# Neighbourhood values with high and low parts side by side as weights, two query tiles at a time, and the fillers' second units in other steps

## The chip, the cores and the metric

One NeuronCore of a Trainium2 chip runs the whole program: TensorE (matmuls, writing to PSUM), VectorE, ScalarE and GpSimd work beside each other, and SyncE issues the DMAs in one in-order queue. Engines meet by semaphores. The metric is the device time of one execution in microseconds (us), the median of several runs; lower is better.

## The reference

Two layers of a mixer with three branches run over 128 context and 1024 latent tokens (1152 in all), width 1024. The branch that matters here is neighbourhood attention with 8 heads of 64:

```python
s_loc = einsum('bhrqd,bhriwd->bhrqiw', qg, kg) * scale + bias   # 8 x 16 window, clamped at the borders
s_loc = where(col_ok, s_loc, NEG_INF)
s_ctx = einsum('bhrqd,bhnd->bhrqn', qg, k_ctx) * scale
p = softmax(concatenate([s_loc, s_ctx], -1))
o = einsum('bhrqiw,bhriwd->bhrqd', p_loc, vg) + einsum('bhrqn,bhnd->bhrqd', p_ctx, v_ctx)
```

Each layer starts with `mod = silu(c) @ w_mod + b_mod`, which scales, shifts and gates the normalised input, and one projection `h @ w_in` feeds queries, keys, values and gates of all branches. All is float32.

## The kernel before

**Exactness.** Every product of two float32 operands is made of three matmuls in the faster f32r form: each operand is split into a high part (a copy rounded to f32r, by ScalarE) and a low part (the rest, by VectorE or GpSimd), and high x high, high x low and low x high are summed in PSUM.

**The neighbourhood phase.** A layer handles its 8 heads as 4 pairs `p`; `u` numbers the pairs of both layers, 0 to 7. A pair has 9 query tiles of 128 tokens, steps `t` = 0 to 8 (8 is the context tile, `LT`). A query tile attends to its own key tile, the two beside it and the cached context tile `TILES`: 3 key tiles for t = 0 and 7, 4 for 1 to 6, 1 for 8. In a step, TensorE turns the probabilities of tile t (`probs_t`, L896 to L902, banks 6 and 7 of PSUM), computes the scores of tile t+1 (L770, L779), runs a unit, multiplies values by probabilities (`values`, L905 to L914, bank 4), and may run a second unit. ScalarE copies the turned probabilities to `pth` (`highs`) and takes exponentials of tile t+1 (`exps`); VectorE makes `ptl` (`lows`), adds the bias, normalises (`biased`, `normed`) and multiplies the output by the gate (`gated`, L1722).

The values of both heads of a pair stand side by side as weights, 128 keys x (64 + 64) channels, `vhi` and `vlo`; the moving operand is the probabilities of both heads, 256 columns. The result is 128 x 256, of which `gated` reads the two 64 x 128 blocks that belong together.

**Units and fillers.** A unit is 24 matmuls of 384 columns (L731), a third of one 128-channel chunk of the big projection. Each head pair carries 5 filler chunks, 15 units numbered 0 to 14 here: q, k, a gate, v and a gate (`qkgvg`) for the next pair, five gates for the last pair. `na_steps` (L109) deals them out: two units in each of steps 0 to 5, one in steps 6 to 8. ScalarE evacuates a unit (`evacuate`), and after a chunk's third unit copies the high part of a later weight chunk (L1143); GpSimd makes the low part (L1999).

**Modulations.** In layer 0, each of steps 0 to 7 of each pair also runs one of the next 32 modulation products: `modulation` (L790) on the buffer `mraw` before the unit, ScalarE copies the row, `modulation_sums` folds it (L796) after the unit. `mraw` is one buffer of 512 KB.

**SyncE's queue.** SyncE walks over the pair's five fillers. For filler j it first issues a weight load (L495), then modulation loads up to a fixed number, each behind the use of the load before, and then what the chunk's result needs:

```python
for j, c in enumerate(fillers(l, "na", p)):
    weights_to(CHUNK[c] + 3)
    if l + 1 < DEPTH:
        mod_to(MOD_STEPS * p + (3, 4, 6, 7, 8)[j])
    keep_streaming(c)
```

`keep_streaming` (L511) waits for the evacuation of the chunk's third unit, `unit_evac(c, NC - 1)`, if the chunk is k, v or a gate, and issues its store (L518, L523). `MOD_STEPS` is 8, so the load for step 7 is issued at j = 4, behind the store of the fourth filler, whose third unit is unit 11.

Of the kernel before, what the change touches and what calls it, by code (L numbers as in the profile page):

```python
# [8 lines left out]
F32 = mybir.dt.float32  # L9
# [202 lines left out]
def build(nc, x_in, cache_na_k, cache_na_v, cache_diff_k, cache_diff_v, cvec, norm_g, w_mod,  # L212
# [66 lines left out]
    kh = pl("kh", [P, TK], F32R)  # L279
    kl = pl("kl", [P, TK], F32R)  # L280
    vhi = pl("vhi", [P, TILES + 1, P], F32R)
    vlo = pl("vlo", [P, TILES + 1, P], F32R)
    vraw = pl("vraw", [P, P])
    gst_at = pl.at
# [113 lines left out]
    def group(g):  # L398

        return ps[:, 3 * g:3 * g + NC, 0:CH]  # L400

    def by_chunk(ap):
        return ap.rearrange("p (c n) -> p c n", n=CH)
# [4 lines left out]
        un_done u_evac z_tanh z_evac  # L408
        na_s na_b na_e na_p na_pt na_pth na_ptc na_pv na_o df_s df_m df_e df_p df_pt df_pth df_ptc df_pv df_o
        f_store0 f_store1 u_pair pair_copied folded x_done q_done q_copied f_hi f_lo f_ctx  # L410
# [69 lines left out]
    with nc.Block() as block:  # L480
# [3 lines left out]
        def _(sp):  # L484
# [70 lines left out]
            for l in range(DEPTH):  # L555
# [9 lines left out]
                for p in range(HEADS):  # L565
# [23 lines left out]

                    sp.wait_ge(S.na_o, TILES * (u + 1))  # L590
                    sp.dma_start(outs_dram[0, p], obuf[:]).then_inc(S.o_store, 16)
# [106 lines left out]
        def _(pe):  # L698
# [157 lines left out]
            for l in range(DEPTH):  # L856
# [17 lines left out]
                for p in range(HEADS):  # L874
# [46 lines left out]
                    unit(z, 0)  # L921
                    pe.wait_ge(S.na_o, TILES * u)
                    values_to_rows(n, v, 1, 4)
# [8 lines left out]
                    for t, units in enumerate(na_steps(l, p)):  # L932
                        probs_t(t, 0)
                        probs_t(t, 1)
                        if t + 1 < TILES:
                            scores(t + 1)
                        mod = l + 1 < DEPTH and t < MOD_STEPS
                        if mod:
                            modulation(MOD_STEPS * p + t)
                        unit(*units[0])  # L940
                        if mod:
                            modulation_sums(MOD_STEPS * p + t)
                        values(t)
                        if len(units) > 1:
                            unit(*units[1])
# [39 lines left out]
                job(("u", l, "fn", 0), hhi, hlo)  # L985
                pe.wait_ge(S.na_o, TILES * HEADS * (l + 1))
                if l + 1 < DEPTH:
# [141 lines left out]
        def _(act):  # L1129
# [69 lines left out]

            def cached_high(n):  # L1200
                act.wait_ge(S.vc_load, 16 * (n + 1))
                fn(vhi[:, TILES, :], vraw[:], ACT.Copy).then_inc(S.vc_hi, 1)

            def value_high(n, i, bank):

                a, b = 4 * i, min(4 * i + 4, TILES)
                act.wait_ge(S.v_done, 3 * n + i + 1)
                fn(vhi[:, a:b, :], ps[:, bank, 0:(b - a) * P].rearrange("p (t n) -> p t n", n=P), ACT.Copy
                   ).then_inc(S.v_hi, 1)
# [62 lines left out]
            for l in range(DEPTH):  # L1272
# [26 lines left out]
                for p in range(HEADS):  # L1299
# [10 lines left out]
                    def highs(t, e):  # L1310

                        n = len(na_tiles(t))
                        act.wait_ge(S.na_pt, u0 + 2 * t + e + 1)
                        if e == 0 and t >= 2:

                            act.wait_ge(S.na_pv, TILES * u + t - 1)
                        fn(pth[:, t % 2, 0:n, e, :], ps[:, 6 + e, 0:n * P].rearrange("p (t n) -> p t n", n=P), ACT.Copy  # L1317
                           ).then_inc(S.na_pth, 1)

                    if p:  # L1320
                        act.wait_ge(S.na_pv, TILES * u)
                    cached_high(n)
                    value_high(n, 0, 5)
                    if p:
                        act.wait_ge(S.na_o, TILES * u)
                    evacuate(z, 0)
                    value_high(n, 1, 4)
                    evacuate(z, 1)
                    value_high(n, 2, 5)
# [214 lines left out]
        def _(dve):  # L1544
# [84 lines left out]
            for l in range(DEPTH):  # L1629
# [45 lines left out]

                def value_low(n, i, bank):

                    a, b = 4 * i, min(4 * i + 4, TILES)
                    dve.wait_ge(S.v_hi, 3 * n + i + 1)
                    v.tensor_tensor(vlo[:, a:b, :], ps[:, bank, 0:(b - a) * P].rearrange("p (t n) -> p t n", n=P),  # L1680
                                    vhi[:, a:b, :].bitcast(F32), ALU.subtract).then_inc(S.v_lo, 1)

                for p in range(HEADS):
# [24 lines left out]
                    def lows(t, e):  # L1708

                        n = len(na_tiles(t))  # L1710
                        dve.wait_ge(S.na_pth, u0 + 2 * t + e + 1)
                        v.tensor_tensor(ptl[:, t % 2, 0:n, e, :], ps[:, 6 + e, 0:n * P].rearrange("p (t n) -> p t n", n=P),  # L1712
                                        pth[:, t % 2, 0:n, e, :].bitcast(F32), ALU.subtract).then_inc(S.na_ptc, 1)
# [12 lines left out]
                    value_low(n, 0, 5)  # L1726
                    silu_unit(z, 0)
                    value_low(n, 1, 4)
# [4 lines left out]
                    value_low(n, 2, 5)  # L1733
                    normed(0, 0)
                    normed(0, 1)
                    silu_unit(z, 2)
                    for t in range(TILES):
# [7 lines left out]
                        if l + 1 < DEPTH and t < MOD_STEPS:  # L1745
# [242 lines left out]
        def _(pool):  # L1988
# [26 lines left out]
            for l in range(DEPTH):  # L2015
# [8 lines left out]

                def cached_low(n):
                    pool.wait_ge(S.vc_hi, n + 1)
                    g_.tensor_tensor(vlo[:, TILES, :], vraw[:], vhi[:, TILES, :].bitcast(F32), ALU.subtract
                                     ).then_inc(S.vc_lo, 1)
# [5 lines left out]
                for p in range(HEADS):  # L2034
                    n, cs = n0 + p, fillers(l, "na", p)
                    split_to(SPLIT_NO[cs[0]] + 1)
                    cached_low(n)
                    split_to(SPLIT_NO[cs[-1]] + 2)
# [152 lines left out]
```

## Time and profile before

| | us |
|---|---|
| median of 3 runs | 2887.7 |
| lowest, highest | 2886.08, 2890.15 |
| the profiled execution | 2886.48 |
| its span in the trace | 2884.7 |

The neighbourhood phases lie at about 100 to 522 us (layer 0) and 1514 to 1930 us (layer 1). In the rows below a line names the start and duration in us, the engine, the source line, the operation and its tiles (out<-in), and shapes. Matmuls are pipelined: the recorded duration of one is longer than the distance between two starts, and the distance is what one costs when they follow each other.

### The profile page before, as it was taken

The page shows a single profiled execution, that of the slowest core. Times are in us where ns is not written, and L with a number is a line of the kernel's source. Part 1 is how long each engine was busy: PE and PEld are TensorE (multiplying, and loading weights), DVE is VectorE, ACT ScalarE, POOL GpSimd, SP SyncE. Part 2 cuts the span into 40 slices and gives each one's busy share as a digit, 9 for nine tenths or more (in the row PEclk, how much of TensorE's full clock was granted, in tenths as well). Part 3 has the DMA queues.
Part 4 walks back from the last instruction along what each step waited for, and adds up shares of the span by engine and source line. Part 5 has one row for each costly group of instructions (what it writes and reads, how often), then busy time and mean ns, then how long its engine had stood idle before and what let it go on. Part 6 is the DMA issues. An engine that isn't in the chain of part 4 may idle for free.

```text
span 2884.7 us, 43952 instructions
## 1 busy us (share of the span) xinstructions
PE 2824.3 (98%) x18284; PEld 2712.9 (94%) x18284; DVE 1341.0 (46%) x2349; ACT 1070.2 (37%) x1963; POOL 614.3 (21%) x312
## 2 busy tenths in 40 slices
PE   6999999999999999999999999999999999999998
PEld 4999999999999989999999999999999989999997
DVE  4343444233657575446344434423156567554643
ACT  4333333322444444422343433423234444533132
POOL 0221221133121212122431221213222221211141
PEclk9999999999999999999999999999999999999999
DMA  5332233202111112254422120221211111215532
GB/s 213 113 113 74 105 100 111 84 26 84 41 42 47 49 33 96 88 205 139 127 88 67 67 84 32 84 83 35 75 34 48 49 42 47 88 48 188 167 108 94
DMA packets 83702, 246.57 MB, mean 85 GB/s; under 512 B 9136, under 2 KB 30128, under 8 KB 82480
## 3 DMA queue, kind: packets, MB, share of 16 engines
q1 hardware_dynamic: 83504, 243.76, 24.9%
q8 instruction: 145, 2.38, 0.3%
q14 instruction: 53, 0.43, 0.0%
HBM read 189.72 MB, written 54.00 MB: 84 GB/s over the span
## 4 chain that ended last, share of the span: by engine, by line
PE 90%; DVE 5%; ACT 2%; DMA 1%; issue 1%; SPq 0%; DVEq 0%; POOL 0%; POOLq 0%; ACTq 0%
PE ps L731 45%; PE ps L714 19%; PE ps L834 6%; PE ps L770 5%; PE ps L914 3%; PE ps L1057 3%; PE ps L1048 2%; PE ps L902 2%; PE ps L977 1%; DVE e L1882 1%; DVE stat L1865 1%; ACT e L1456 1%; DMA wmod<-w_mod 1%; DVE aTl L1889 1%; PE ps L790 1%
## 5 line engine op out<-in xcount | busy, mean ns | idle before, releaser
L731 PE MATMUL ps<-hhi,whi 128*128 128x384 f32 x2640 | 915.7, 347 | 5.7 <-DVE obuf L1897 3.3
L731 PE MATMUL ps<-hhi,wlo 128*128 128x384 f32 x2640 | 885.6, 335 | 0.0
L731 PE MATMUL ps<-hlo,whi 128*128 128x384 f32 x2640 | 883.1, 335 | 0.0
L1999 POOL TENSOR_TENSOR wlo<-wraw,whi 128x1024 fp32r<-128x1024 f32 (+1 forms) x188 | 415.9, 2213 | 2010.3 <-ACT whi L1143 2010.3
L731 PEld LDWEIGHTS ps<-hhi,whi 128*128 128x128 f32 x2640 | 499.5, 189 | 37.2 <-issue 23.4
L731 PEld LDWEIGHTS ps<-hlo,whi 128*128 128x128 f32 x2640 | 496.4, 188 | 0.9
L731 PEld LDWEIGHTS ps<-hhi,wlo 128*128 128x128 f32 x2640 | 495.4, 188 | 0.0
L1143 ACT ACTIVATE whi<-wraw 128x1024 fp32r<-128x1024 f32 (+1 forms) x188 | 174.5, 928 | 224.4 <-PE ps L714 206.5
L1465 ACT ACTIVATE aTh<-ps 128x512 fp32r<-128x512 f32 (+1 forms) x200 | 96.5, 482 | 273.3 <-PE ps L1048 273.3
L1712 DVE TENSOR_TENSOR ptl<-ps,pth 128x512 fp32r<-128x512 f32 (+1 forms) x144 | 82.1, 612 | 246.8 <-ACT pth L1317 246.6
L1865 DVE TENSOR_REDUCE stat<-ps 128x1 f32<-128x1152 f32 x144 | 176.6, 1231 | 13.8 <-PE ps L770 13.4
L1456 ACT ACTIVATE e<-ps,stat 128x1152 f32<-128x1152 f32 x144 | 162.4, 1128 | 55.0 <-DVE stat L1865 55.0
L1168 ACT ACTIVATE gst<-ps 128x384 f32<-128x384 f32 x144 | 70.5, 490 | 262.9 <-PE ps L731 262.9
L1889 DVE TENSOR_TENSOR aTl<-ps,aTh 128x512 fp32r<-128x512 f32 (+1 forms) x200 | 108.4, 542 | 103.6 <-ACT aTh L1465 102.8
L1307 ACT ACTIVATE sn<-sn,stat 128x512 f32<-128x512 f32 (+1 forms) x144 | 95.8, 665 | 112.5 <-DVE stat L1697 106.5
L714 PE MATMUL ps<-omh,whi 128*128 128x384 f32 x576 | 132.4, 337 | 0.0
L714 PE MATMUL ps<-omh,wlo 128*128 128x384 f32 x576 | 131.6, 336 | 0.0
L714 PE MATMUL ps<-oml,whi 128*128 128x384 f32 x576 | 131.5, 336 | 0.0
L1048 PE MATMUL ps<-ident,e 128*128 128x128 f32 x584 | 100.5, 279 | 12.2 <-DVE aTl L1889 9.7
L770 PE MATMUL ps<-kh,qh 64*128 64x384 f32 (+2 forms) x560 | 103.8, 366 | 0.0
L714 PEld LDWEIGHTS ps<-omh,whi 128*128 128x128 f32 x576 | 103.1, 188 | 0.5
L714 PEld LDWEIGHTS ps<-omh,wlo 128*128 128x128 f32 x576 | 103.3, 188 | 0.0
(217 smaller groups left out, 4788.5 us busy)
## 6 DMA issues: line engine op xcount, KB each, us to landing
wraw<-w_in SPq DMA_DIRECT2D x128, 512.0 KB, 4.3
gates_dram<-gst SPq DMA_DIRECT2D x48, 576.0 KB, 3.0
gth<-gates_dram SPq DMA_DIRECT2D x48, 576.0 KB, 4.7
mraw<-w_mod SPq DMA_DIRECT2D x32, 512.0 KB, 3.9
wraw<-w_branch SPq DMA_DIRECT2D x48, 256.0 KB, 2.8
bias<-rpb SPq DMA_DIRECT2D x8, 1280.0 KB, 6.0
outs_dram<-obuf SPq DMA_DIRECT2D x16, 576.0 KB, 4.0
oraw<-outs_dram SPq DMA_DIRECT2D x16, 576.0 KB, 3.8
```

Source lines behind the costliest of these rows:

```text
L714: x = mm(ps[:, at + n, 0:CH], a[:, s % 2, k, :], b[k][:, n * CH:(n + 1) * CH], start=(k == 0 and a is whi and b is mhi), stop=(k == kt - 1 ...
L731: x = mm(ps[:, bank, 0:CH], a[:, s % 2, k, :], b[:, k, n * CH:(n + 1) * CH], start=(k == 0 and a is whi and b is hhi), stop=(k == KT - 1 a ...
L770: x = mm(out, a[r, t * P:(t + 1) * P], b[r, k0:k1], start=(i == 0), stop=(i == 2))
L834: x = mm(ps[:, bank, 0:CH], a[:, k, :], b[:, k, n * CH:(n + 1) * CH], start=(k == 0 and a is hi and b is hhi), stop=(k == KT - 1 and a is lo))
L1048: x = nc.tensor.transpose(ps[:, DF_TURN_BANK[h][t], j * P:(j + 1) * P], e1[:, t % 2, kt * P:(kt + 1) * P], ident[:])
L1143: fn(halves(s)[0][:, 0:kt, :], wraw[:, n % 2, 0:kt, :], ACT.Copy).then_inc(S.w_hi, 1)
L1307: fn(sn[:, e, 0:nk], sn[:, e, 0:nk], ACT.Exp, bias=stat[:, e, 1:2], accum_out=stat[:, e, 3:4]).then_inc(S.na_e, 1)
L1456: fn(out if t == LT else by_chunk(out), group(m) if t < LT else ps[:, 3 * m, 0:nk], ACT.Exp, bias=stat[:, t % 2, m:m + 1], accum_out=stat[ ...
L1465: fn(aTh[:, 4 * g:4 * g + w, (t % 2) * P:(t % 2 + 1) * P], ps[:, DF_TURN_BANK[h][t], 0:w * P].rearrange("p (t n) -> p t n", n=P), ACT.Copy ...
L1865: v.tensor_reduce(stat[:, t % 2, m:m + 1], group(m) if t < LT else ps[:, 3 * m, 0:TC], AX.XY if t < LT else AX.X, ALU.max, negate=True).th ...
L1889: v.tensor_tensor(aTl[at], ps[:, DF_TURN_BANK[h][t], 0:w * P].rearrange("p (t n) -> p t n", n=P), aTh[at].bitcast(F32), ALU.subtract).then ...
L1999: g_.tensor_tensor(lo[:, 0:kt, :], wraw[:, n % 2, 0:kt, :], hi[:, 0:kt, :].bitcast(F32), ALU.subtract).then_inc(S.w_lo, 1)
```

## The change

**Weights and matmuls.** `vhi` and `vlo` become one tensor for this phase, `vparts`: for each key tile 256 columns in four quarters, head 0 high, head 0 low, head 1 low, head 1 high. A matmul now takes the 128 columns of one head (its high and low part) as weights and one part of that head's probabilities, of two query tiles together, as the moving operand. `values(pair)` therefore runs once for steps 0 and 1, 2 and 3, 4 and 5, 6 and 7, at the odd step, and once for step 8. Key tiles that only one of the two query tiles sees are multiplied with 128 columns, the others with 256. The product low x low, which was left out, is now summed too. `pth` and `ptl` hold 9 slots of two query tiles, instead of two buffers.

**Outputs.** High and low sums of a head stand in different halves of the partitions. ScalarE copies one half to the new `vsum` (`spilled`), VectorE adds the other half and multiplies by the gate (`gated`), for two tiles at once, at the even step after. `na_o` and `na_pv` count 5 per head pair (`NA_OUTS`) instead of 9.

**Units.** `NA_TWO` places the second units in steps 0, 2, 3, 4, 6 and 8: the steps hold 2,1,2,2,2,1,2,1,2 units instead of 2,2,2,2,2,2,1,1,1. SyncE's loop is unchanged.

```diff
+NA_TWO = (0, 2, 3, 4, 6, 8)
+NA_OUTS = LT // 2 + 1
+
+
 def na_steps(l, p):
 
     units = [(c, n) for c in fillers(l, "na", p) for n in range(NC)]
-    more, steps = len(units) - TILES, []
+    steps = []
     for t in range(TILES):
-        steps.append([units.pop(0) for _ in range(2 if t < more else 1)])
+        steps.append([units.pop(0) for _ in range(2 if t in NA_TWO else 1)])
...
+def turned_order(t):
+
+    tiles = na_tiles(t)
+    return [0, 1, 3, 2] if t % 2 and len(tiles) == 4 else [*range(len(tiles))]
+
+
+def first_slot(t):
+
+    return 1 if t % 2 or t == 0 else 0
...
+    vparts = nc.alloc_sbuf_tensor_at("vparts", [P, TILES + 1, 2 * P], F32R, offset=v_at)
...
-    pth = pl("pth", [P, 2, 4, 2, P], F32R)
-    ptl = pl("ptl", [P, 2, 4, 2, P], F32R)
+    pth_at = pl.at
+    pth = pl("pth", [P, 9, 2, P], F32R)
+    ptl = pl("ptl", [P, 9, 2, P], F32R)
     csilp = pl("csilp", [P, KT, 32])
-    mrow4 = pl("mrow4", [P, P])
+    mrow4 = nc.alloc_sbuf_tensor_at("mrow4", [P, P], F32, offset=pth_at + TILE_B)
+    vsum = pl("vsum", [P, 2 * P])
...
+        return vparts[:, a:b].rearrange("p t (q n) -> p t q n", n=P // 2)[:, :, 0:4:3, :]
...
+        return vparts[:, a:b].rearrange("p t (q n) -> p t q n", n=P // 2)[:, :, 1:3, :]
...
-                        for j in range(len(na_tiles(t))):
-                            x = nc.tensor.transpose(ps[:, 6 + e, j * P:(j + 1) * P], sn[:, e, j * P:(j + 1) * P], ident[:])
+                        for i, j in enumerate(turned_order(t)):
+                            x = nc.tensor.transpose(ps[:, 6 + e, i * P:(i + 1) * P], sn[:, e, j * P:(j + 1) * P], ident[:])
...
-                    def values(t):
-
-                        pe.wait_ge(S.na_ptc, u0 + 2 * t + 2)
-
-                        if t:
-                            pe.wait_ge(S.na_o, TILES * u + t)
-                        tiles = na_tiles(t)
-                        for j, vtile in enumerate(tiles):
-                            for a, b in ((vhi, pth), (vlo, pth), (vhi, ptl)):
-                                x = mm(ps[:, 4, 0:2 * P], a[:, vtile, :], b[:, t % 2, j], start=(j == 0 and a is vhi and b is pth),
-                                       stop=(j == len(tiles) - 1 and b is ptl))
+                    def values(pair):
+
+                        t = 2 * pair
+                        pe.wait_ge(S.na_ptc, u0 + 2 * min(t + 1, LT) + 2)
+
+                        if pair:
+                            pe.wait_ge(S.na_o, NA_OUTS * u + pair)
+                        if t == LT:
+                            tiles = [(0, LT, 0, P)]
+                        else:
+                            tiles = [(1, t, 0, 2 * P), (2, t + 1, 0, 2 * P), (3, TILES, 0, 2 * P)]
+                            tiles += [(0, t - 1, 0, P)] if t else []
+                            tiles += [(4, t + 2, P, 2 * P)] if t + 2 < LT else []
+                        for e in range(2):
+                            for slot, vtile, a, b in tiles:
+                                for part in (pth, ptl):
+                                    x = mm(ps[:, 4, 2 * P * e + a:2 * P * e + b], vparts[:, vtile, e * P:(e + 1) * P],
+                                           part[:, 4 * e + slot].rearrange("p q n -> p (q n)")[:, a:b],
+                                           start=(slot == tiles[0][0] and part is pth), stop=(slot == tiles[-1][0] and part is ptl))
                         x.then_inc(S.na_pv, 1)
...
-                        values(t)
+                        if t % 2 or t == LT:
+                            values(t // 2)
...
+                    def spilled(pair):
+
+                        w = 2 * P if pair < LT // 2 else P
+                        act.wait_ge(S.na_pv, NA_OUTS * u + pair + 1)
+                        if pair:
+                            act.wait_ge(S.na_o, NA_OUTS * u + pair)
+                        for e in range(2):
+                            own, other = slice(64 * e, 64 * e + 64), slice(64 - 64 * e, 128 - 64 * e)
+                            x = fn(vsum[own, 0:w], ps[other, 4, 2 * P * e:2 * P * e + w], ACT.Copy)
+                        x.then_inc(S.na_spilled, 1)
...
                         highs(t, 0)
                         highs(t, 1)
+                        if t and t % 2 == 0:
+                            spilled(t // 2 - 1)
...
-                        for c, i in units:
+                        for of, (c, i) in enumerate(units):
                             raw_free(c, i)
                             evacuate(c, i)
+                            if t == LT and of == 0:
+                                spilled(LT // 2)
...
-                    def gated(t):
-
-                        dve.wait_ge(S.na_pv, TILES * u + t + 1)
-                        if t == 0 and n:
+                        at = (slice(None), slice(4 * e + first_slot(t), 4 * e + first_slot(t) + n), t % 2 if t < LT else 0)
+                        v.tensor_tensor(ptl[at], ps[:, 6 + e, 0:n * P].rearrange("p (t n) -> p t n", n=P),
+                                        pth[at].bitcast(F32), ALU.subtract).then_inc(S.na_ptc, 1)
+
+                    def gated(pair):
+
+                        w = 2 * P if pair < LT // 2 else P
+                        dve.wait_ge(S.na_spilled, NA_OUTS * u + pair + 1)
+                        if pair == 0 and n:
                             dve.wait_ge(S.o_store, 16 * n)
                         for e in range(2):
-                            r = slice(64 * e, 64 * e + 64)
-                            x = v.tensor_tensor(obuf[r, P * t:P * t + P], ps[r, 4, P * e:P * e + P],
-                                                zs[r, P * t:P * t + P], ALU.mult)
-                        x.then_inc(S.na_o, 1)
-
-                    value_low(n, 0, 5)
+                            own = slice(64 * e, 64 * e + 64)
+                            v.tensor_tensor(vsum[own, 0:w], ps[own, 4, 2 * P * e:2 * P * e + w], vsum[own, 0:w], ALU.add)
+                        dve.drain()
+                        at = slice(2 * P * pair, 2 * P * pair + w)
+                        v.tensor_tensor(obuf[:, at], vsum[:, 0:w], zs[:, at], ALU.mult).then_inc(S.na_o, 1)
...
-                        gated(t)
+                        if t and t % 2 == 0:
+                            gated(t // 2 - 1)
+                    gated(LT // 2)
```

ScalarE, layer 0, second head pair, before: from the evacuation of unit 9 (`vT`) at the end of step 4 to `exps` in step 7. `pth` is `highs`, `sn` is `exps`, `mrow` the modulation's row, `vT`, `qraw`, `gst` the results of v, q and gate units, `whi` a weight chunk's high part.

```order
L1172 ACTIVATE vT<-ps 128x384
L1317 ACTIVATE pth<-ps 128x4x128 x2
L1307 ACTIVATE sn,stat<-sn,stat 128x512 x2
L1341 ACTIVATE mrow_100<-ps 128x128
L1172 ACTIVATE vT<-ps 128x384 x2
L1143 ACTIVATE whi<-wraw 128x1024
L1317 ACTIVATE pth<-ps 128x4x128 x2
L1307 ACTIVATE sn,stat<-sn,stat 128x384 x2
L1341 ACTIVATE mrow_100<-ps 128x128
L1168 ACTIVATE gst_93<-ps 128x384
L1317 ACTIVATE pth<-ps 128x3x128 x2
L1307 ACTIVATE sn,stat<-sn,stat 128x128 x2
```

And after: steps 6 and 7 of the same pair.

```order
L1365 ACTIVATE pth<-ps 128x4x128 x2
L1378 ACTIVATE vsum<-ps 64x256 x2
L1354 ACTIVATE sn,stat<-sn,stat 128x384 x2
L1402 ACTIVATE mrow_101<-ps 128x128
L1209 ACTIVATE vT<-ps 128x384 x2
L1180 ACTIVATE whi<-wraw 128x1024
L1365 ACTIVATE pth<-ps 128x3x128 x2
L1354 ACTIVATE sn,stat<-sn,stat 128x128 x2
L1402 ACTIVATE mrow_101<-ps 128x128
```

The last two `vT` evacuations (units 10 and 11) stood in step 5, ahead of the `pth` of step 6; now they stand behind the `mrow` of step 6, ahead of the `pth` of step 7. The `vsum` copies are new, between `pth` and `sn`.

TensorE, layer 0, first head pair, before: the end of a unit in step 1, the folding matmul and the value matmuls of that one tile (12 in all).

```order
L731 MATMUL ps<-hhi,wlo 128x384
L796 MATMUL ps<-fold_101,mrow_100 128x2
L914 MATMUL ps<-pth,vhi 128x256
L914 MATMUL ps<-pth,vlo 128x256
L914 MATMUL ps<-ptl,vhi 128x256
```

And after: the folding matmul of step 1 and the value matmuls of tiles 0 and 1 together (16 in all).

```order
L824 MATMUL ps<-fold_103,mrow_101 128x2
L949 MATMUL ps<-pth,vparts 128x256
L949 MATMUL ps<-ptl,vparts 128x256
...
L949 MATMUL ps<-pth,vparts 128x128
L949 MATMUL ps<-ptl,vparts 128x128
L949 MATMUL ps<-pth,vparts 128x256
L949 MATMUL ps<-ptl,vparts 128x256
```

Both parts of the probabilities now pass through the same weights, and the matmuls of a key tile that one query tile sees are 128 columns wide.

## Rows read from the trace of the kernel before

**Rows 1.** The page's first part: span, then busy us, share, instructions.

```profile
span 2884.7 us, 43952 instructions
...
PE 2824.3 (98%) x18284; PEld 2712.9 (94%) x18284; DVE 1341.0 (46%) x2349; ACT 1070.2 (37%) x1963; POOL 614.3 (21%) x312
```

**Rows 2.** Busy time by stretch, second head pair; columns as in the first line.

```profile
core 0: us, PE busy (x) PEld busy (x) DVE busy (x) ACT busy (x) POOL busy (x), PEclk, DMA share, GB/s
...
203.00:312.00 109.00, 109.00 (x834) 104.32 (x833) 44.23 (x141) 40.84 (x93) 20.48 (x9) 1.00 0.29 98
```

**Rows 3.** TensorE in order of time, end of step 6 and step 7, first pair.

```profile
183.99 0.28 PE L796 MATMUL ps<-fold,mrow 128*128 128x2 f32 x2
184.12 0.36 PE L914 MATMUL ps<-pth,vhi 128*128 128x256 f32 x1
184.32 0.28 PE L914 MATMUL ps<-pth,vlo 128*128 128x256 f32 x1
...
185.62 0.82 PE L902 MATMUL ps<-ident,sn 128*128 128x128 f32 x6
186.37 0.33 PE L770 MATMUL ps<-kh,qh 64*128 64x128 f32 x2
...
186.85 0.65 PE L790 MATMUL ps<-mraw,csilp 128*32 128x128 f32 x16
```

**Rows 4.** TensorE in order of time, the last value group of the differential attention.

```profile
2612.55 0.22 PE L1057 MATMUL ps<-aTh,vhi 128*128 128x128 f32 x1
2612.61 0.27 PE L1057 MATMUL ps<-aTh,vlo 128*128 128x128 f32 x1
2612.72 0.28 PE L1057 MATMUL ps<-aTl,vhi 128*128 128x128 f32 x1
2612.84 0.75 PE L714 MATMUL ps<-omh,whi 128*128 128x384 f32 x3
```

**Rows 5.** TensorE in order of time, end of layer 0's neighbourhood phase.

```profile
525.74 0.28 PE L914 MATMUL ps<-pth,vhi 128*128 128x256 f32 x1
525.86 0.28 PE L914 MATMUL ps<-pth,vlo 128*128 128x256 f32 x1
...
526.49 0.79 PE L714 MATMUL ps<-hhi,whi 128*128 128x384 f32 x3 [0.23 <-ACT gst L1168]
```

**Rows 6.** ScalarE and VectorE in order of time, steps 5 and 6.

```profile
177.71 0.49 ACT L1172 ACTIVATE vT<-ps 128x384 f32<-128x384 f32 x1 [5.37 <-PE ps L731]
...
181.69 0.61 ACT L1307 ACTIVATE sn<-sn,stat 128x384 f32<-128x384 f32 x1 [1.57 <-DVE stat L1697]
...
183.47 0.42 DVE L1705 TENSOR_SCALAR sn<-sn,stat 128x384 f32<-128x384 f32 x1
```

**Rows 7.** The chain that ended last, in order of time: start, us, what.

```profile
202.94 4.19 PE ps L731 x24
```

**Rows 8.** TensorE's and SyncE's queue in order of time, steps 5 and 6.

```profile
177.45 1.03 PE L902 MATMUL ps<-ident,sn 128*128 128x128 f32 x8
...
179.14 0.63 PE L790 MATMUL ps<-mraw,csilp 128*32 128x128 f32 x14
...
178.23 0.34 SPq L523 DMA_DIRECT2D new_na_v<-vT  x1
178.62 0.43 SPq L495 DMA_DIRECT2D wraw<-w_in  x1
179.84 0.33 SPq L531 DMA_DIRECT2D mraw<-w_mod  x1
```

**Rows 9.** DMA issues from 129, 179, 397, 203 us: KB, us to landing.

```profile
mraw<-w_mod SPq DMA_DIRECT2D x1, 512.0 KB, 3.4
...
mraw<-w_mod SPq DMA_DIRECT2D x1, 512.0 KB, 4.4
...
mraw<-w_mod SPq DMA_DIRECT2D x1, 512.0 KB, 5.2
...
mraw<-w_mod SPq DMA_DIRECT2D x1, 512.0 KB, 8.4
```

**Rows 10.** TensorE after an idle stretch; then by stretch: length, busy (x), PEclk.

```profile
42.91 1.30 PE L748 MATMUL ps<-hhi,whi 128*128 128x384 f32 x3 [5.48 <-DVE hlo L1640]
...
42.91:45.87 2.96, 2.96 (x9) 0.51 0.02 6
45.87:47.47 1.60, 1.60 (x11) 1.00 0.00 0
```

More of the change, by code:

```diff
@@ L106, in gate_no @@
     return c[1] * 3 * KT + c[3]
+NA_TWO = (0, 2, 3, 4, 6, 8)
+NA_OUTS = LT // 2 + 1
 def na_steps(l, p):
     units = [(c, n) for c in fillers(l, "na", p) for n in range(NC)]
-    more, steps = len(units) - TILES, []
+    steps = []
     for t in range(TILES):
-        steps.append([units.pop(0) for _ in range(2 if t < more else 1)])
+        steps.append([units.pop(0) for _ in range(2 if t in NA_TWO else 1)])
+    assert not units
     return steps
@@ L280, in build @@
     kl = pl("kl", [P, TK], F32R)
+    v_at = pl.at
     vhi = pl("vhi", [P, TILES + 1, P], F32R)
     vlo = pl("vlo", [P, TILES + 1, P], F32R)
+    vparts = nc.alloc_sbuf_tensor_at("vparts", [P, TILES + 1, 2 * P], F32R, offset=v_at)
     vraw = pl("vraw", [P, P])
@@ L400, in group, with v_high, v_low @@
         return ps[:, 3 * g:3 * g + NC, 0:CH]
+    def v_high(a, b):
+        return vparts[:, a:b].rearrange("p t (q n) -> p t q n", n=P // 2)[:, :, 0:4:3, :]
+    def v_low(a, b):
+        return vparts[:, a:b].rearrange("p t (q n) -> p t q n", n=P // 2)[:, :, 1:3, :]
     def by_chunk(ap):
@@ L588, in _ @@
                                 sp.dma_start(tab_t[i][:], dft_t[:, i]).then_inc(S.tab_load, 16)
[L590 removed]
+                    sp.wait_ge(S.na_o, NA_OUTS * (u + 1))
                     sp.dma_start(outs_dram[0, p], obuf[:]).then_inc(S.o_store, 16)
@@ L921, in _ @@
                     unit(z, 0)
-                    pe.wait_ge(S.na_o, TILES * u)
+                    pe.wait_ge(S.na_o, NA_OUTS * u)
                     values_to_rows(n, v, 1, 4)
@@ L985, in _ @@
                 job(("u", l, "fn", 0), hhi, hlo)
-                pe.wait_ge(S.na_o, TILES * HEADS * (l + 1))
+                pe.wait_ge(S.na_o, NA_OUTS * HEADS * (l + 1))
                 if l + 1 < DEPTH:
@@ L1198, in key_high, with by_head, cached_high, value_high @@
                 fn(kh[:], kraw[:], ACT.Copy).then_inc(S.x_hi, 1)
-            def cached_high(n):
+            def by_head(ap):
+                return ap.rearrange("p (t e n) -> p t e n", e=2, n=P // 2)
+            def cached_high(n, ph="df"):
                 act.wait_ge(S.vc_load, 16 * (n + 1))
-                fn(vhi[:, TILES, :], vraw[:], ACT.Copy).then_inc(S.vc_hi, 1)
-            def value_high(n, i, bank):
+                if ph == "na":
+                    fn(v_high(TILES, TILES + 1), by_head(vraw[:]), ACT.Copy).then_inc(S.vc_hi, 1)
+                else:
+                    fn(vhi[:, TILES, :], vraw[:], ACT.Copy).then_inc(S.vc_hi, 1)
+            def value_high(n, i, bank, ph="df"):
                 a, b = 4 * i, min(4 * i + 4, TILES)
                 act.wait_ge(S.v_done, 3 * n + i + 1)
+                if ph == "na":
+                    fn(v_high(a, b), by_head(ps[:, bank, 0:(b - a) * P]), ACT.Copy).then_inc(S.v_hi, 1)
+                    return
                 fn(vhi[:, a:b, :], ps[:, bank, 0:(b - a) * P].rearrange("p (t n) -> p t n", n=P), ACT.Copy
@@ L1313, in highs @@
                         act.wait_ge(S.na_pt, u0 + 2 * t + e + 1)
-                        if e == 0 and t >= 2:
-                            act.wait_ge(S.na_pv, TILES * u + t - 1)
-                        fn(pth[:, t % 2, 0:n, e, :], ps[:, 6 + e, 0:n * P].rearrange("p (t n) -> p t n", n=P), ACT.Copy
+                        if e == 0 and t >= 2 and t % 2 == 0:
+                            act.wait_ge(S.na_pv, NA_OUTS * u + t // 2)
+                        at = 4 * e + first_slot(t)
+                        fn(pth[:, at:at + n, t % 2 if t < LT else 0, :], ps[:, 6 + e, 0:n * P].rearrange("p (t n) -> p t n", n=P), ACT.Copy
                            ).then_inc(S.na_pth, 1)
                     if p:
-                        act.wait_ge(S.na_pv, TILES * u)
-                    cached_high(n)
-                    value_high(n, 0, 5)
+                        act.wait_ge(S.na_pv, NA_OUTS * u)
+                    def spilled(pair):
[7 more added lines that the diff above has]
+                        x.then_inc(S.na_spilled, 1)
+                    cached_high(n, "na")
+                    value_high(n, 0, 5, "na")
                     if p:
-                        act.wait_ge(S.na_o, TILES * u)
+                        act.wait_ge(S.na_o, NA_OUTS * u)
                     evacuate(z, 0)
-                    value_high(n, 1, 4)
+                    value_high(n, 1, 4, "na")
                     evacuate(z, 1)
-                    value_high(n, 2, 5)
+                    value_high(n, 2, 5, "na")
                     exps(0, 0)
@@ L1674, in silu_unit, with value_low @@
                                            op0=ALU.add, op1=ALU.mult).then_inc(S.z_evac, 1)
-                def value_low(n, i, bank):
+                def value_low(n, i, bank, ph="df"):
                     a, b = 4 * i, min(4 * i + 4, TILES)
                     dve.wait_ge(S.v_hi, 3 * n + i + 1)
+                    if ph == "na":
+                        v.tensor_tensor(v_low(a, b), ps[:, bank, 0:(b - a) * P].rearrange("p (t e n) -> p t e n", e=2, n=P // 2),
+                                        v_high(a, b).bitcast(F32), ALU.subtract).then_inc(S.v_lo, 1)
+                        return
                     v.tensor_tensor(vlo[:, a:b, :], ps[:, bank, 0:(b - a) * P].rearrange("p (t n) -> p t n", n=P),
@@ L1732, in _ @@
                     biased(0, 1)
-                    value_low(n, 2, 5)
+                    value_low(n, 2, 5, "na")
                     normed(0, 0)
@@ L2023, in key_low, with cached_low @@
                     g_.tensor_tensor(kl[:], kraw[:], kh[:].bitcast(F32), ALU.subtract).then_inc(S.x_split, 1)
-                def cached_low(n):
+                def cached_low(n, ph="df"):
                     pool.wait_ge(S.vc_hi, n + 1)
+                    if ph == "na":
+                        g_.tensor_tensor(v_low(TILES, TILES + 1), vraw[:].rearrange("p (t e n) -> p t e n", e=2, n=P // 2),
+                                         v_high(TILES, TILES + 1).bitcast(F32), ALU.subtract).then_inc(S.vc_lo, 1)
+                        return
                     g_.tensor_tensor(vlo[:, TILES, :], vraw[:], vhi[:, TILES, :].bitcast(F32), ALU.subtract
@@ L2036, in _ @@
                     split_to(SPLIT_NO[cs[0]] + 1)
-                    cached_low(n)
+                    cached_low(n, "na")
                     split_to(SPLIT_NO[cs[-1]] + 2)
```

7 lines of the change are left out of this document (3 added, 4 removed).

## The prediction

> **What bounds the kernel now.** I read the page's busy shares first: TensorE is busy for 98% of the span, VectorE for 46%, ScalarE for 37% [rows 1]. Then I took a stretch of the neighbourhood phase and asked each engine's busy time in it: in 109 us of the second head pair TensorE has no idle time at all and runs at its full granted clock [rows 2]. So in the phase that the change touches, every matmul's turn on TensorE is paid for in full, and work of the other engines is free until it makes TensorE wait. The last thing that I looked for was therefore not busy time but the queue that feeds each of TensorE's waits, and what that queue itself waits for.
>
> **TensorE's own work.** Before, a head pair has 31 (query tile, key tile) pairs: 3 + 6x4 + 3 + 1. Three matmuls of 256 columns each make 93. In the timeline they start 0.118 us apart ((185.62 - 184.32) / 11) [rows 3], so 93 x 0.118 = 10.97 us. After, a pair of heads has 76: 16, 20, 20, 16 and 4. Of these 48 are 256 columns wide and 28 are 128 wide. The wide ones cost 48 x 0.118 = 5.66 us.
>
> The narrow ones are the unknown. The only 128-column matmuls of this kind in the trace are three of the differential attention: starts 0.06, 0.11 and 0.12 us apart [rows 4]. The first follows a 384-column matmul, behind which weights can be loaded early; the other two show the steady state, 0.115 on average, hardly under the 0.118 of a 256-column one. The 128-column transposes come 0.125 apart (six from 185.62 to 186.37) [rows 3]. In the new code at most four narrow ones stand in a row, each with a weight load of its own, so I take 0.115: 28 x 0.115 = 3.22. That is 8.88 us, a saving of 2.09 per head pair, **-16.7 us** over eight. Bounds: at 0.125 the saving is 14.5, at 0.06 it is 29.0.
>
> The Trainium skill ("TensorE: Matmul & The Clock Gate", Back-to-back issue gap) gives about 81 ns between 128-column matmuls in a stream with weight loads, well under the 115 ns seen here. By it the saving would be about 24.3 us.
>
> The first matmul of a group takes 0.20 instead of 0.118 (184.12 to 184.32) where it stands behind the small folding matmul L796 [rows 3]; where none stands there the group starts without it [rows 5]. In layer 0 that surcharge passes to whatever follows the folding matmul, and I count nothing; if it vanished in the 16 even steps, 1.3 us more would be saved.
>
> At the end of each layer's phase three value matmuls used to stand between the last unit and the wait for its evacuation: 525.74 to 526.49 with 0.23 idle [rows 5]. Now they stand ahead of that unit, and the same 0.75 us is waited through empty, so 3 x 0.12 = 0.36 of the saving is lost twice: **+0.7 us**.
>
> **The other engines.** ScalarE gets two copies of 64x256 per pair of tiles ahead of exps. There it stood idle for 1.57 us [rows 6], and a PSUM read of 384 columns takes 0.49, so two of 256 fit: nothing. If that cover were gone, up to 1 us would be added in 32 steps. VectorE has two adds and one product per pair instead of four halves of a product; it ends its work for step 7 at 183.89 (183.47 + 0.42), 1.7 us before TensorE asks for it at 185.62 [rows 3, 6]. Steps without value matmuls now hold a second unit of 4.19 us [rows 7], so this margin grows. The gating of pair 3 is needed by the last value matmuls in step 8 and has the unit of 4.19 us in front of them: nothing.
>
> **What is moved past SyncE's queue.** This is the term that decides. In layer 0 each of steps 0 to 7 runs one modulation matmul group on `mraw`, a single buffer. Its load is issued by SyncE in one fixed order, shared with stores that wait for evacuations. The load for step 7 stands behind `keep_streaming` of the fourth filler, which waits for that chunk's third unit, number 11 counted from 0. Before, two units in each of steps 0 to 5 put unit 11 at the end of step 5, and the load had all of step 6 to wait out and land in. After, the counts 2,1,2,2,2,1,2,1,2 put unit 11 last in step 6, directly ahead of step 7. SyncE's order has not changed; the change moves what it waits for.
>
> The same sequence stands in the trace one step earlier. TensorE leaves unit 11 at 177.45, the store is issued at 178.23, the weights at 178.62, taking 0.43 [rows 8]. The modulation load behind them would go out 1.65 us after unit 11 has ended ((178.62 + 0.43) + 0.05 - 177.45); there it waited until 179.84 for step 6's modulation, which cost nothing. TensorE wants it in step 7 after six transposes and a short score group: 186.85 - 185.62 = 1.23 us after the step's start [rows 3]. So TensorE waits 1.65 + L - 1.23 = L + 0.42, with L the time from issue to landing.
>
> L is 3.4 us for such a load alone, 4.4 and 5.2 where a weight load went out 1.2 us before, 8.4 where the 1280 KB bias load went too [rows 9]. Here the weight load goes out 0.48 before, so more of the two overlaps: from the mean of 4.4 and 5.2 I add half a microsecond and take 5.3. The wait is 5.72 us, four times (one per head pair of layer 0): **+22.9 us**. Bounds: 3.4 gives 15.3, 8.4 gives 35.3. Nothing is waiting to be gained behind it: in step 7 TensorE has already done its transposes and scores.
>
> A wait of this length may cost clock. After TensorE's 5.48 us of idling the granted clock was 0.51, that is the 1.2 GHz level, over the nine matmuls that followed: 2.96 us where the next stretch of about nine took 1.60 [rows 10]. That is 1.4 us. There light work stood ahead of the idling, here dense work does, so I count it for half: 4 x 0.7 = **+2.8 us**, between 0 and 5.6.
>
> **Sum.** -16.7 + 0.7 + 22.9 + 2.8 = +9.7 us, against the profiled execution's own 2886.5: 2896.2. The median of the runs is 1.2 above that execution, so 2897.4, a ratio of 1.003. What this kernel's measurement can tell from no change is about 0.2%, 5.8 us.
>
> **Rivals.**
> 1. The narrow matmuls run at their streaming rate. For it: the first spacing of 0.06 [rows 4]. Against: the next two. Saving 12.3 us more: 2885.1, no difference. With the skill's 81 ns, named above, it would be about 2889.8, also no difference.
> 2. The load lands as fast as alone, and the clock holds. 3.4 + 0.42 = 3.82, four times 15.3: 2887.7 - 16.0 + 15.3 = 2887.0. For it: the rows' smallest landing; against: a weight load is always ahead.
> 3. Not slower but faster: the load is not late. It decides at the point where the load lands within 1.23 us of step 7's start, which would need SyncE to be free of the wait for unit 11, or another load ahead of it that frees the buffer sooner. Against: the buffer is one, the queue one. It gives 2887.7 - 16.0 = 2871.7.
> 4. A second load is late too, that for step 4. It stands behind unit 5, which moves from the end of step 2 to the middle of step 3. After unit 5 come 0.87 + 0.78 until issue; ahead of TensorE lie 20 value matmuls (2.4), unit 6 (4.2) and 1.69 of step 4 (179.14 - 177.45) [rows 8], so a load with L = 5.3 has some 1.3 us to spare. At 8.4 it would be 1.8 late, and step 7's wait would grow as well, by 3.1: 4 x 4.9 = 19.6, 2917.
>
> **How the numbers follow.** My forecast has 0.77: 2897.4, its own range 2890 to 2906 (L of 4.4 without loss of clock gives -16.0 + 19.3 = +3.3, 2891; L of 6.5 with the whole clock loss gives -16.0 + 27.7 + 5.6 = +17.3, 2905). Rival 1 has 0.07, rival 2 0.05, rival 3 0.07, rival 4 0.04. A tenth of the forecast's share lies under +5.8 us. Faster by over 0.2%: rival 3 and a little of 1, 0.08. Within 0.2%: the rest of 1, rival 2 and 0.10 of the forecast, 0.20. Slower: 0.72. The range of 2885 to 2906 leaves out rival 3 and the upper end.
>
> **What would show it.** In the profile after, TensorE's waits should hold a row with the modulation line as the waiter and the DMA of `mraw` as the releaser, 4 times and some 23 us. Layer 1, which has no modulations, should be shorter by 8 us, and layer 0's phase longer by some 17. The value group should show 608 matmuls with 128-column spacings near 0.115, and ScalarE's `vsum` copies should make nobody wait. No such wait row would make the prediction wrong; a row with half the time would make L or the clock wrong.

## The result and the profile after

The changed kernel takes 2901.2 us (median, 2899.8 to 2903.0) against 2888.3: a ratio of 1.0045, 95% interval 1.0031 to 1.0059. It is 12.9 us slower. The profiled execution's span grew from 2884.7 to 2899.4 us. Three single executions among the runs below took 3039.8, 3123.7 and 10744 us, far above the others of their kernels; no ratio and no median given here contains them.

The page and the list of TensorE's waits show both halves of the story. First the page of the changed kernel, as [rows 1]:

```profile
span 2899.4 us, 43752 instructions
...
PE 2818.2 (97%) x18148; PEld 2706.0 (93%) x18148; DVE 1343.8 (46%) x2325; ACT 1101.0 (38%) x2043; POOL 614.9 (21%) x312
```

TensorE has 136 matmuls less, eight times 17, and is busy for 6.1 us less, although part of its work ran at a lower clock. The span grew all the same, so it must have waited. Its waits (engine, tile and line, what it waited for: us in total, times, longest):

```profile
PE ps L818 <- DMA mraw<-w_mod: 20.6, 4, 5.8
PE ps L871 <- DVE sq L1689: 16.3, 2, 14.9
PE ps L1085 <- DVE aTl L1961: 9.2, 10, 1.1
...
PE ps L742 <- ACT gst L1205: 1.2, 2, 0.6
```

The first row is new: four waits of the modulation matmuls on the load of `mraw`. The second belongs to the start of the program and the third to the differential attention; both were there before, with 16.7 and 9.7 us. The last is the end of each layer's neighbourhood phase, 0.5 us in total before and 1.2 now.

Where the new wait stands is seen in TensorE's order of time, first head pair, end of step 6 and step 7. It answers to [rows 3]:

```profile
177.88 0.34 PE L759 MATMUL ps<-hhi,wlo 128*128 128x384 f32 x1
178.06 0.82 PE L930 MATMUL ps<-ident,sn 128*128 128x128 f32 x6
178.81 0.33 PE L798 MATMUL ps<-kh,qh 64*128 64x128 f32 x2
...
184.24 1.08 PE L818 MATMUL ps<-mraw,csilp 128*32 128x128 f32 x16 [4.89 <-DMA mraw<-w_mod]
185.25 0.69 PE L759 MATMUL ps<-hhi,whi 128*128 128x384 f32 x1
185.74 0.52 PE L759 MATMUL ps<-hlo,whi 128*128 128x384 f32 x1
...
190.67 0.34 PE L759 MATMUL ps<-hhi,wlo 128*128 128x384 f32 x1
190.85 0.34 PE L759 MATMUL ps<-hhi,whi 128*128 128x384 f32 x1
```

Unit 11 is the last unit of step 6, and step 7 begins at 178.06. Transposes and scores are done at once, then nothing until 184.24. The matmuls of the next unit start 0.32 us apart (185.74 to 186.06) where 0.175 is usual, until about 190.2. The same stretch in SyncE's queue, with ScalarE's evacuation of unit 11, answers to [rows 8]:

```profile
178.32 0.49 ACT L1209 ACTIVATE vT<-ps 128x384 f32<-128x384 f32 x1 [3.96 <-PE ps L759]
...
178.83 0.34 SPq L551 DMA_DIRECT2D new_na_v<-vT  x1
179.22 0.43 SPq L523 DMA_DIRECT2D wraw<-w_in  x1
179.70 0.43 SPq L559 DMA_DIRECT2D mraw<-w_mod  x1
```

The load goes out at 179.70, 1.64 us after the step began, as soon as SyncE gets to it. Before, at the same place of the queue, it was held until 179.84 by step 6's modulation [rows 8], and then had the rest of step 6 to land in. Now it lands in 4.5 us (DMA issues of 178 to 180 us; KB, us to landing), as [rows 9]:

```profile
mraw<-w_mod SPq DMA_DIRECT2D x1, 512.0 KB, 4.5
```

The granted clock in four stretches that begin with step 7's modulation, in the pairs 1 to 4 (length, busy, clock as a share of 2.4 GHz), as [rows 10]. Only the first ends at the folding matmul; the others run 0.23 to 1.13 us past it, so their lengths can't be compared with each other:

```profile
184.24:191.90 7.66, 7.66 (x41) 0.60 0.00 0
299.36:307.00 7.64, 7.64 (x51) 0.76 0.00 0
413.24:421.00 7.76, 7.76 (x43) 0.62 0.01 2
529.10:537.00 7.90, 7.90 (x43) 0.62 0.00 0
```

And by stretch over a whole pair of layer 0 and over most of one of layer 1, as [rows 2]:

```profile
208.00:323.00 115.00, 110.02 (x827) 105.05 (x826) 45.32 (x140) 46.17 (x105) 20.33 (x9) 0.97 0.28 98
1533.00:1620.00 87.00, 87.00 (x585) 84.16 (x584) 37.56 (x109) 35.60 (x77) 12.39 (x6) 1.00 0.17 56
```

The stretch of layer 1, which has no modulations, is busy throughout. From the first transposes of a layer's neighbourhood phase to the end of its last wait (for `gst`), layer 0 took 423.7 us before (102.81 to 526.49) and takes 446.0 now (102.50 to 548.51), 22.3 more. Layer 1 took 398.0 (1527.80 to 1925.76) and takes 389.4 (1550.12 to 1939.51), 8.6 less. The whole loss stands in layer 0. These lengths leave out what differs between executions before the phase begins, and are used beside the medians below.

### The profile page after: what moved, and what is told of

It reads as the page before. It is cut to its first block, busy times and chain, and to the rows that moved or that the text cites. A ratio compares the mean times of both kernels' runs of the same rounds, so it can differ in the third digit from the quotient of the medians.

```text
span 2899.4 us, 43752 instructions
## 1 busy us (share of the span) xinstructions
PE 2818.2 (97%) x18148; PEld 2706.0 (93%) x18148; DVE 1343.8 (46%) x2325; ACT 1101.0 (38%) x2043; POOL 614.9 (21%) x312
## 4 chain that ended last, share of the span: by engine, by line
PE 90%; DVE 5%; ACT 2%; DMA 2%; issue 1%; SPq 1%; DVEq 0%; POOL 0%; POOLq 0%; ACTq 0%
PE ps L759 46%; PE ps L742 18%; PE ps L862 6%; PE ps L798 5%; PE ps L1094 3%; PE ps L949 2%; PE ps L1085 2%; PE ps L930 2%; PE ps L1014 1%; DVE e L1954 1%; DVE stat L1937 1%; PE ps L818 1%; DMA wmod<-w_mod 1%; DMA mraw<-w_mod 1%; DVE aTl L1961 1%
## 5 line engine op out<-in xcount | busy, mean ns | idle before, releaser
L1937 DVE TENSOR_REDUCE stat<-ps 128x1 f32<-128x1152 f32 x144 | 176.6, 1231 | 13.8 <-PE ps L798 13.5
L742 PE MATMUL ps<-omh,whi 128*128 128x384 f32 x576 | 132.5, 338 | 0.0
L742 PE MATMUL ps<-omh,wlo 128*128 128x384 f32 x576 | 131.6, 336 | 0.0
L742 PE MATMUL ps<-oml,whi 128*128 128x384 f32 x576 | 131.6, 336 | 0.0
L742 PEld LDWEIGHTS ps<-omh,whi 128*128 128x128 f32 x576 | 103.1, 188 | 0.5
L742 PEld LDWEIGHTS ps<-omh,wlo 128*128 128x128 f32 x576 | 103.3, 188 | 0.0
```

What stands on the lines that cost most here:

```text
L742: x = mm(ps[:, at + n, 0:CH], a[:, s % 2, k, :], b[k][:, n * CH:(n + 1) * CH], start=(k == 0 and a is whi and b is mhi), stop=(k == kt - 1 ...
L1937: v.tensor_reduce(stat[:, t % 2, m:m + 1], group(m) if t < LT else ps[:, 3 * m, 0:TC], AX.XY if t < LT else AX.X, ALU.max, negate=True).th ...
```

## The experiments

**1. The load issued ahead of the wait.** One number of SyncE's table is changed, so that the load for step 7 is issued at the fourth filler, ahead of `keep_streaming`'s wait for unit 11.

```diff
-                            mod_to(MOD_STEPS * p + (3, 4, 6, 7, 8)[j])
+                            mod_to(MOD_STEPS * p + (3, 4, 6, 8, 8)[j])
```

> The changed kernel with one number changed: SyncE issues the modulation load for step 7 at the fourth filler, ahead of the wait for that filler's third unit, instead of at the fifth. Late-load theory: the four waits of 20.6 us on the load go, and with them the time at the half clock (about 10 us), so 2870 to 2872. Rival, the two added copies and sums per pair of tiles cost time on TensorE's path: only part of it comes back, 2880 or more.

Measured: 2872.4 us, ratio to the kernel before 0.9945 (0.9932 to 0.9958), 28.8 us under the changed kernel. SyncE's queue in the first pair (the second of the two loads waits for step 6's modulation, and both stand ahead of the store):

```profile
161.41 9.38 SPq L559 DMA_DIRECT2D mraw<-w_mod  x2
179.78 0.34 SPq L551 DMA_DIRECT2D new_na_v<-vT  x1
```

No wait on `mraw` is left, and step 7 from modulation to folding takes 4.84 us instead of 7.66, at full clock:

```profile
180.23:185.07 4.84, 4.84 (x42) 1.00 0.42 122
```

The time falls as the late-load theory says: layer 0's phase is 415.2 us long (103.44 to 518.67), 30.8 less than in the changed kernel, and layer 1's is 389.4 as there. The rival, a price of the added copies and sums, is out: with the load in time TensorE and its weight loads wait for neither in these phases. This version beats both kernels.

**2. The second units back in steps 0 to 5.** The value part of the change alone.

```diff
-NA_TWO = (0, 2, 3, 4, 6, 8)
+NA_TWO = (0, 1, 2, 3, 4, 5)
```

> The changed kernel with the second units back in steps 0 to 5. Late-load theory: unit 11 ends in step 5 again and no load is late. But step 6 now holds one unit and no value matmuls, some 6.2 us in layer 1, where VectorE's share of a step took 6.4 us before the change: up to 1 us of wait in each of 8 pairs. 2871 to 2879, and TensorE's waits name the normalisation, not the load. Rival, the load is late because of contention and not because of the order: waits on it remain, 2890 or more.

Measured: 2874.6 us, ratio 0.9953 (0.9939 to 0.9967). The waits on the load are gone but for one of 0.2 us, as expected. The waits on the normalisation came too, in layer 1 only and smaller than the 1 us allowed for; they stand in the list of the weight loads (PEld), not in that of the matmuls:

```profile
PEld ps L930 <- DVE sn L1772: 1.0, 4, 0.3
PEld ps L818 <- DMA mraw<-w_mod: 0.7, 2, 0.4
PE ps L818 <- DMA mraw<-w_mod: 0.2, 1, 0.2
```

Step 6 of a pair in layer 1, TensorE's start and VectorE's two normalisations, and the start of step 7:

```profile
1590.27 1.03 PE L930 MATMUL ps<-ident,sn 128*128 128x128 f32 x8
...
1595.49 0.42 DVE L1772 TENSOR_SCALAR sn<-sn,stat 128x384 f32<-128x384 f32 x1
...
1596.28 0.42 DVE L1772 TENSOR_SCALAR sn<-sn,stat 128x384 f32<-128x384 f32 x1
...
1596.25 1.05 PE L930 MATMUL ps<-ident,sn 128*128 128x128 f32 x6
```

The second normalisation ends at 1596.70, 6.4 us after the step began, and the step is 5.98 us long. The transposes of the first head cover part of the rest. The six transposes then take 0.98 us to the scores at 1597.23, against 0.75 in experiment 1. The new placement of the second units avoids this. From step 0 of one pair to step 0 of the next, a pair of layer 1 takes 100.80 us in experiment 1 and 101.07 here. The medians, 2.2 us apart with overlapping intervals, can't show so little by themselves. The price of the new placement, below, takes 0.4 us a layer back.

**3. Only the units moved.** The kernel before, with its second units in steps 0, 2, 3, 4, 6 and 8, and nothing else.

```diff
-        steps.append([units.pop(0) for _ in range(2 if t < more else 1)])
+        steps.append([units.pop(0) for _ in range(2 if t in (0, 2, 3, 4, 6, 8) else 1)])
```

> The kernel before with only the second units moved to steps 0, 2, 3, 4, 6 and 8. Late-load theory: the full loss without the gain, 4 waits of about 5.2 us and 2.5 to 3 us each at the half clock, about 2888.3 + 31 = 2919 (2914 to 2922). Rival, the loss comes from the value part of the change: 2888, no difference.

Measured: 2918.2 us, ratio 1.0098 (1.0082 to 1.0114). The full loss without the gain, as expected. The same kernel was run once more for its profile.

> The kernel before with only the second units moved, again, for its profile: four waits on the modulation load of about 5 us each, granted clock at its lower level behind each of them, 2914 to 2922.

Measured: 2919.1 us in this single execution, and in TensorE's waits:

```profile
PE ps L790 <- DMA mraw<-w_mod: 21.1, 4, 6.3
```

The granted clock is 0.50 in the 4.84 us behind the first of these waits. From modulation to folding the four pairs take 7.15, 6.81, 6.61 and 7.53 us, 8.7 in all above 4.84 each. With the waits that is 29.8 us; layer 0's phase is 30.3 us longer than before (103.46 to 557.45).

**4. The wait filled with work.** The changed kernel with 42 matmuls of 256 columns ahead of step 7's modulation; their results are used by nobody.

```diff
+                        if mod and t == MOD_STEPS - 1:
+                            pe.wait_ge(S.mr_added, MOD_STEPS * p + t)
+                            for _ in range(42):
+                                mm(ps[:, 5, 2 * P:4 * P], hhi[:, 0, 0:P], hhi[:, 0, 0:2 * P], start=True, stop=True)
```

> The changed kernel with 42 extra matmuls of 256 columns (unused results) ahead of step 7's modulation in layer 0, 42 x 0.118 = 4.96 us, about the length of the wait. If the half clock after the wait comes from TensorE's idling, it goes and the waits shrink to under 1 us each: 2901.2 less about 10 = 2891 (2889 to 2893). If the clock falls for another reason, nothing changes: 2901.

Measured: 2892.7 us, ratio 1.0013 (1.0004 to 1.0023). The extra work (first pair; then modulation to folding) and the one wait that is left:

```profile
177.91:183.13 5.22, 5.22 (x44) 1.00 0.56 213
183.13:187.98 4.85, 4.85 (x42) 1.00 0.01 3
...
PE ps L818 <- DMA mraw<-w_mod: 1.0, 1, 1.0
```

TensorE was kept from the next unit for as long as in the changed kernel: 4 x 5.2 + 1.0 = 21.9 us of extra work and wait against 20.6 of wait. Yet the kernel is 8.6 us faster, because the stretch behind runs at full clock, 4.85 instead of 7.66 us. So the lower level came from TensorE's idling, and cost 8.6 + 21.9 - 20.6 = 9.9 us. The timeline of the changed kernel gives the same: modulation to folding took 7.66, 6.51, 7.53 and 7.59 us in the four pairs against 4.84 each, 9.9 in total.

**5. The load ahead of the weight load.** Still behind the wait for unit 11, but first of the two.

```diff
+                        if l + 1 < DEPTH and j == 4:
+                            mod_to(MOD_STEPS * p + 8)
                         weights_to(CHUNK[c] + 3)
-                        if l + 1 < DEPTH:
+                        if l + 1 < DEPTH and j < 4:
                             mod_to(MOD_STEPS * p + (3, 4, 6, 7, 8)[j])
                         keep_streaming(c)
```

> The changed kernel with the modulation load for step 7 issued ahead of the weight load instead of behind it, still behind the wait for unit 11's evacuation. It goes out 0.48 us earlier and alone lands in 3.4 to 3.8 us instead of 4.5: the wait shrinks from 5.2 to about 3.8 us, 4 x 1.4 = 5.6 us less. With the half clock unchanged 2895.6; if a wait of 3.8 us costs less clock or none, 2886 to 2892. If the wait were set by something other than this load's landing, it would stay at 2901.

Measured: 2895.4 us, ratio 1.0022 (1.0012 to 1.0032), 5.8 us under the changed kernel.

```profile
181.49 0.34 SPq L551 DMA_DIRECT2D new_na_v<-vT  x1
181.88 0.43 SPq L559 DMA_DIRECT2D mraw<-w_mod  x1
...
PE ps L820 <- DMA mraw<-w_mod: 15.5, 4, 4.3
```

The waits shrank from 20.6 to 15.5 us, 1.3 each. The landing of this load (3.8 us) sets the wait. Waits of 3.7 to 4.3 us lower the clock too. In the first pair, TensorE in order of time:

```profile
185.70 0.65 PE L820 MATMUL ps<-mraw,csilp 128*32 128x128 f32 x16 [3.69 <-DMA mraw<-w_mod]
186.28 0.66 PE L761 MATMUL ps<-hhi,whi 128*128 128x384 f32 x1
186.74 0.52 PE L761 MATMUL ps<-hlo,whi 128*128 128x384 f32 x1
...
192.13 0.28 PE L826 MATMUL ps<-fold,mrow 128*128 128x2 f32 x2
```

Here the modulation itself still ran at full speed (0.65, against 1.08 in the changed kernel and in this one's last pair, whose wait was 4.33), and the first part of the unit behind it at half. From modulation to folding it is 6.43, and 6.4 in the other pairs, against 4.84: 6.3 us in total, 3.6 less than in the changed kernel. The two terms make 21.8 us. Layer 0's phase confirms it: 437.3 us (105.16 to 542.45), 22.1 more than in experiment 1 and 8.7 less than in the changed kernel (5.1 of waits, 3.6 of clock). The medians show 5.8 of these 8.7 and the spans 4.2; the rest lies outside the phase, which in the profiled executions began at 105.16 here and at 102.50 there.

**6. The units moved and the load early, on the kernel before.** Experiment 3 with the table of experiment 1.

> The kernel before with the second units in steps 0, 2, 3, 4, 6 and 8 and the load for step 7 issued at the fourth filler. If the place of the second units costs only through the late load, this is the kernel before in time: 2888 (2886 to 2890), against 2918 without the early load. If moving the units has a price of its own, 2891 or more.

Measured: 2889.3 us, ratio 1.0002 (0.9993 to 1.0011). Moving the units costs nothing by itself that the times can show (at the end of each phase the wait for `gst` is 0.4 us longer, as in the changed kernel); experiment 3's 30 us went through the late load.

## Why the prediction was right, point by point

The forecast was 2897.4 us, slower, with 2885 to 2906 around it; 2901.2 was measured, 12.9 us over the kernel before where the sum had 9.7. The mechanism was right. The size of one term, the clock, was not, and that the total still came close was in part luck: the late load was taken 2.3 us too dear, which hid a third of the 7.1 us missing in the clock. With the clock at its measured size the sum would have given 2904.5, still inside the range.

**The late load, +22.9 foreseen, 20.6 measured.** The step was right in place and count, and near in size. The load was issued 1.64 us into step 7 (1.65 foreseen) and landed in 4.5 us (5.3 taken): the half microsecond that I had added for the nearer weight load was not there. The waits are 4.89, 4.98, 4.88 and 5.84 us. In the last pair the load took 5.5 us to land; there the chunk is a gate, and its store of 576 KB goes ahead instead of one of 64 KB. That the store is the reason was not tested.

**The clock, +2.8 foreseen, 9.9 measured.** This is the term that was mis-sized. I took 1.4 us from the one idle stretch of [rows 10], as a maximum, and half of it. There the lower level ended some 3 us after the matmuls had begun again. Here, by the matmuls' spacing, it lasted 3.4 us in the second pair and 5.7 to 6.0 in the others, 1.7 to 2.8 us of loss each. What sets the length was not found. My bound of 5.6 was taken from a single case and was no bound.

**TensorE's own work, -16.7 foreseen, about -17.7.** The pitch of the head pairs in layer 0 was 109.45 us before (from 178.23 to 287.68, the stores of `new_na_v`) and is 107.26 in experiment 1 (179.78 to 287.04): 2.19 us saved per pair where 2.09 were foreseen. In layer 1, from step 0 to step 0, it went from 103.03 to 100.80, 2.23 saved. The value groups of one pair of layer 1 sum to 10.89 us before and 8.52 now, where 10.97 and 8.88 were foreseen; the narrow matmuls were cheaper. In a group of 20 of layer 1:

```profile
1584.67 0.28 PE L949 MATMUL ps<-pth,vparts 128*128 128x256 f32 x1
...
1585.37 0.22 PE L949 MATMUL ps<-pth,vparts 128*128 128x128 f32 x1
1585.43 0.28 PE L949 MATMUL ps<-ptl,vparts 128*128 128x128 f32 x1
1585.55 0.28 PE L949 MATMUL ps<-pth,vparts 128*128 128x128 f32 x1
1585.66 0.28 PE L949 MATMUL ps<-ptl,vparts 128*128 128x128 f32 x1
1585.77 0.33 PE L949 MATMUL ps<-pth,vparts 128*128 128x256 f32 x1
1585.94 0.28 PE L949 MATMUL ps<-ptl,vparts 128*128 128x256 f32 x1
...
1586.92 0.39 PE L759 MATMUL ps<-hhi,whi 128*128 128x384 f32 x1
```

The group takes 2.25 us. With 12 wide ones at 0.118 that leaves 0.104 for a narrow one, against 0.115 taken. A part of this is lost right behind the group, where a 384-column matmul takes 0.23 (1586.92 to 1587.15) instead of 0.175. The pattern is that of [rows 4]: the first narrow one passes in 0.06, the next in 0.11 to 0.12, and the wide one behind them takes 0.17, as if it paid back what the first had borrowed. By the Trainium skill ("TensorE: Matmul & The Clock Gate", LDWEIGHTS (loading the stationary operand)) a weight load takes its columns divided by 1.2 ns, 107 ns for 128; the trace comes near it, since four narrow ones and the wide one behind them take 0.114 each ((1585.94 - 1585.37) / 5). No run here changes the number of weight columns, so that the weight load sets this pace is not shown. The 81 ns of the same page's section "Back-to-back issue gap" were not reached.

In layer 0 the groups of a pair shrink by 2.79 us (11.66 to 8.87 in experiment 1) and the pitch by only 2.19: the surcharge behind the folding matmul passed to what now follows it, as the prediction counted it.

**The end of the phase, +0.7 foreseen:** the row L742 <- `gst` went from 0.5 to 1.2 us. It comes from the placement: 0.4 in experiment 2, 1.2 in experiment 6.

**The other engines, nothing foreseen:** experiment 1 shows no wait of TensorE on them. ScalarE's two copies and VectorE's sums stand in gaps. With the second units in their old steps VectorE's normalisation is late, by 0.26 us in each pair of layer 1 (experiment 2).

The four terms as measured give -17.7 + 0.7 + 20.6 + 9.9 = +13.5. The two phases together grew by 13.8 us (22.3 - 8.6), the spans by 14.7 and the medians by 12.9; the remaining 0.9 of the spans lies outside the phases. The prediction's own signs came out so: the wait row with 4 waits and 20.6 us (some 23 foreseen), layer 1 shorter by 8.6 (8), layer 0 longer by 22.3 (some 17, short mainly by the clock). One sign did not hold to the letter: VectorE waits for ScalarE's `vsum` copies, 25.8 us in 16 waits, but no wait of TensorE comes of it.

**The rivals.** Narrow matmuls at their streaming rate: only the first of each row. The load as fast as alone: no, 4.5 us against 3.4; even issued first (experiment 5, 3.8 us) it cost 21.8 us with the clock. The load not late: false for this change, but its price was right, 2871.7 foreseen and 2872.4 measured when the load was issued early. A second late load, for step 4: not seen, the new wait row counts four and all stand in step 7. The prediction's shares have a small slip: with 0.10 of the forecast its parts add up to 0.21 for no difference and 0.71 for slower, where it says 0.20 and 0.72.

## What to carry to other kernels

Before units of work are moved between steps, list everything that waits for each unit's completion, the DMA queue first: an in-order queue carries that wait to every transfer behind it, also to those that have nothing to do with the unit. A saving on the bounding engine and a late transfer are then of the same order, and the repair can be one number in the queue's table. A wait of a few microseconds on TensorE should be priced with the clock behind it, here half as much again. And a change in one phase is read most sharply from that phase's length in the traces: between the profiled executions here, the phase began anywhere from 101.1 to 105.2 us.

## What the runs showed of the hardware that I had not expected

- Waits of 3.7 to 5.8 us in dense work (the changed kernel and experiment 5) lowered TensorE's granted clock from 2.4 to 1.2 GHz for part of the unit behind them, and cost 1.5 to 2.8 us each beside the wait. A gap of 1.05 us did not (experiment 4, last pair), and the long gaps filled with matmuls cost none of that (experiment 4). The level can fall as late as after the matmuls have begun again: in experiment 5, behind waits of 3.7 us, the modulation of 0.65 us still ran at full speed.
- A 512 KB load behind another of 512 KB, issued 0.48 us earlier, landed in 4.5 us; with 1.2 us between them it had been 4.4 to 5.2 [rows 9]. The nearer neighbour did not slow it beyond that.
- Between 256-column matmuls, a single pair of 128-column ones costs 0.17 us together (192.83 to 193.00 in the changed kernel's first pair), but the next wide one is late by 0.05, which makes 0.11 each against the 0.118 of a wide one: half the columns save little in such a row.
